# Threshold searches in groups of three tiles, two on ScalarE and one on VectorE

## The reference, cut to what matters

```
rel   = relu(einsum('bthd,bsd->bths', iq, ik_all))          # 8 index heads of 64
score = einsum('bths,bth->bts', rel, iw)
score = where(k_pos <= q_pos, score, -inf)
_, sel = lax.top_k(score, n_sel)                            # n_sel = min(256, t // 4)
```

## Time and profile before

| | us |
|---|---|
| median of 3 runs | 4327.86 |
| lowest and highest run | 4326.69, 4332.43 |
| the profiled execution's own time | 4345.04 |
| its span, first to last instruction | 4343.6 |
| channel block, from the trace's timeline | about 220 to 1,225 |

### The profile page before, as it was taken

One profiled execution on the slowest core, in us unless ns is written; L12 is line 12 of the kernel. 1 busy time (PEld: TensorE's weight loads), 2 busy tenths in 40 slices (PEclk: granted clock), 3 DMA queues, 4 the chain that ended last, 5 costly groups with the idle time before them and its releaser, 6 DMA issues. The chain is left out here.

```text
span 4343.6 us, 52016 instructions
## 1 busy us (share of the span) xinstructions
PE 3868.5 (89%) x19882; PEld 3152.5 (73%) x19882; DVE 2196.6 (51%) x4366; ACT 1532.5 (35%) x2446; POOL 653.1 (15%) x530
## 2 busy tenths in 40 slices
PE   7998887788859867888898889899999999979999
PEld 4554554455448546787887878799999999958787
DVE  6648988988953485343444334444444444320200
ACT  2135655565735333333333322322222222221211
POOL 0000000000000002322233210011111111034443
PEclk9998999999979678898899989999999999989999
DMA  3342212120142201111111124211112111064433
GB/s 112 93 98 56 77 43 72 34 72 30 49 145 89 80 9 45 32 37 27 44 39 45 32 66 136 83 40 49 49 39 59 39 48 49 29 209 136 131 121 108
DMA packets 287498, 298.52 MB, mean 69 GB/s; under 512 B 33871, under 2 KB 231375, under 8 KB 282410
## 3 DMA queue, kind: packets, MB, share of 16 engines
q1 hardware_dynamic: 264254, 249.46, 20.3%
q10 hardware_dynamic: 20944, 25.59, 1.7%
q0 software_dynamic: 2112, 20.97, 1.3%
HBM read 202.15 MB, written 94.10 MB: 68 GB/s over the span
## 5 line engine op out<-in xcount | busy, mean ns | idle before, releaser
L538 PE MATMUL chan_p_g<-ht,w_chan 128*128 128x412 f32 (+1 forms) x1760 | 677.4, 528 | 53.4 <-ACT chan_flat L586 33.7
L949 PE MATMUL up_p_g<-ht_high,up_wh 128*128 128x412 f32 (+1 forms) x1760 | 617.3, 351 | 0.0
L949 PE MATMUL up_p_g<-ht_low,up_wh 128*128 128x412 f32 (+1 forms) x1760 | 615.3, 350 | 0.0
L949 PE MATMUL up_p_g<-ht_high,up_wl 128*128 128x412 f32 (+1 forms) x1760 | 615.0, 349 | 0.0
L538 PEld LDWEIGHTS chan_p_g<-ht,w_chan 128*128 128x128 f32 x1760 | 341.5, 197 | 300.8 <-issue 233.4
L970 ACT ACTIVATE up_pre<-up_p_g 128x412 f32<-128x412 f32 (+1 forms) x220 | 113.2, 515 | 738.1 <-PE up_p_g L949 738.1
L1348 ACT ACTIVATE chan_signed<-chan_sc,chan_trial 128x512 bf16<-128x512 f32 (+6 forms) x224 | 304.9, 1361 | 148.6 <-DVE chan_trial L1403 127.8
L1038 DVE TENSOR_SCALAR up_acc<-up_pre,up_taps 128x2048 f32<-128x2048 f32 x44 | 59.3, 1347 | 557.4 <-ACT up_pre L970 557.4
L949 PEld LDWEIGHTS up_p_g<-ht_high,up_wh 128*128 128x128 f32 x1760 | 331.5, 188 | 1.6 <-POOL up_wl L1006 0.4
L949 PEld LDWEIGHTS up_p_g<-ht_low,up_wh 128*128 128x128 f32 x1760 | 331.3, 188 | 1.2
L949 PEld LDWEIGHTS up_p_g<-ht_high,up_wl 128*128 128x128 f32 x1760 | 331.2, 188 | 0.5
(11 more groups left out here) (561 smaller groups left out, 7042.6 us busy)
## 6 DMA issues: line engine op xcount, KB each, us to landing
down_a<-scratch_act SPq DMA_DIRECT2D x88, 512.0 KB, 3.7
scratch_act<-up_acc SPq DMA_DIRECT2D x22, 1028.0 KB
up_w<-in_w_up SPq DMA_DIRECT2D x44, 512.0 KB, 6.4
chan_iq<-scratch_iq SPq DMA_DIRECT2D x28, 512.0 KB, 7.2
scratch_qkv<-chan_acc SPq DMA_DIRECT2D x12, 1028.0 KB, 4.6
keys_of_raw<-scratch_qkv SPq DMA_DIRECT2D x16, 768.0 KB, 5.3
w_chan<-in_w_in SPq DMA_DIRECT2D x22, 512.0 KB, 4.5
proj_x<-in_x_prompt SPq DMA_DIRECT2D x16, 512.0 KB, 4.1
```

Of the source, the lines that this page charges most:

```text
L538: last = pe.matmul(p_g[u % BANKS][:, 0:cols.stop - cols.start], weights[:, k, :], K.ht[:, k, cols], start=(k == 0), stop=(k == KD - 1))
L949: last = pe.matmul(p_g[u][:, 0:cols.stop - cols.start], wp[s][:, k, :], hp[:, k, cols], start=(k == 0 and m == 0), stop=(k == KD - 1 and m ...
```

## The change

`Select` takes groups in place of pairs: `TRIPLES` is one group of two tiles and four of three. The first tile of each group is searched on VectorE, the one or two others on ScalarE, one Sign behind the other, with one signal after the last. The flags of ScalarE's tiles are formed in one operation against the constants in `bound`. `sc` has three buffers; the tile `signed`, to which the Sign wrote what nobody reads, is gone: the first Sign of a step writes to `left`, the second to `order`, which is half as long as before. So the running sum of a wide tile is made in two halves of at most 1,024 columns, the second against the rest of the limit. ScalarE waits for the stores of the group before ahead of its first Sign. `w_step` is set anew; the total of the weights is 859.5.

```diff
+TRIPLES = ((2, 3), (4, 5, 6), (7, 8, 9), (10, 11, 12), (13, 14, 15))
...
-        sel = Select(c, K, range(1, PAIRED), s_iqst, lambda t: (((t + 1) * P - 1) // WIDTH + 1) * 32)
+        sel = Select(c, K, TRIPLES, s_iqst, lambda t: (((t + 1) * P - 1) // WIDTH + 1) * 32)
...
-    RING = 3
+    RING, HALF = 3, SEQ // 2
...
-        self.sc = two("sc", [P, SEQ])
-        self.tie, self.signed = c.sb("tie", [P, SEQ], BF16), c.sb("signed", [P, SEQ], BF16)
-        self.order = c.sb("order", [P, SEQ])
-        self.left = c.sb("left", [P, SEQ], BF16)
+        self.sc = [c.sb(f"sc{i}", [P, SEQ]) for i in range(3)]
+        self.tie, self.left = c.sb("tie", [P, SEQ], BF16), c.sb("left", [P, SEQ], BF16)
+        self.order = c.sb("order", [P, self.HALF])
...
-    w_step = staticmethod(lambda p: 1.0 + 2.3 * (2 * p + 1) / 16)
+    w_step = staticmethod(lambda group: 0.8 + 2.2 * sum(t + 1 for t in group[1:]) / 16)
...
+            if q:
+                act.wait_ge(self.s_out, 16 * self.nth(group[0]))
             for m in range(32):
-                act.wait_ge(S["tried"], (p - self.pairs[0]) * 33 + m + 1)
-                act.activation(self.signed[:, 0:nk], self.sc[1][:, 0:nk], ACT.Sign, scale=-1.0,
-                               bias=self.trial[:, 1:2].bitcast(F32), accum_out=self.signs[:, :]).then_inc(S["signs"], 1)
-                yield self.w_step(p)
+                act.wait_ge(S["tried"], q * 33 + m + 1)
+                for b in range(1, len(group)):
+                    nk = (group[b] + 1) * P
+                    junk = self.left[:, 0:nk] if b == 1 else self.order[:, :].bitcast(BF16)[:, 0:nk]
+                    last = act.activation(junk, self.sc[b][:, 0:nk], ACT.Sign, scale=-1.0,
+                                          bias=self.trial[:, b:b + 1].bitcast(F32), accum_out=self.signs[:, b - 1:b])
+                last.then_inc(S["signs"], 1)
+                yield self.w_step(group)
...
+            for b in range(1, g):
+                dve.memset(self.bound[:, b - 1:b], float((group[b] + 1) * P - 2 * NSEL))
...
-                step(dve.tensor_scalar(miss[:, 1:2], signs[:, :], float(nb - 2 * NSEL), None, ALU.is_gt))
+                step(dve.tensor_tensor(miss[:, 1:g], signs[:, 0:g - 1], self.bound[:, 0:g - 1], ALU.is_gt))
...
-                    dve.scalar_tensor_tensor(out=trial[:, :], in0=miss[:, :], scalar=bit, in1=other[:, :],
+                    dve.scalar_tensor_tensor(out=trial[:, 0:g], in0=miss[:, 0:g], scalar=bit, in1=other[:, 0:g],
                                              op0=ALU.logical_shift_left, op1=ALU.bitwise_xor).then_inc(S["tried"], 1)
...
-                if b == 1:
+                if b:
...
-                step(dve.tensor_tensor_scan(order, tie, tie, 0.0, ALU.add, ALU.bypass))
-                step(dve.scalar_tensor_tensor(out=tie, in0=order, scalar=count[:, b:b + 1], in1=tie, op0=ALU.is_gt, op1=ALU.mult))
+                limit = count[:, b:b + 1]
+                for first in range(0, nk, self.HALF):
+                    part = self.tie[:, first:min(first + self.HALF, nk)]
+                    order = self.order[:, 0:min(self.HALF, nk - first)]
+                    step(dve.tensor_tensor_scan(order, part, part, 0.0, ALU.add, ALU.bypass))
+                    if first + self.HALF < nk:
+                        dve.tensor_tensor(self.rest[:, :], limit, self.order[:, self.HALF - 1:], ALU.subtract)
+                    step(dve.scalar_tensor_tensor(out=part, in0=order, scalar=limit, in1=part, op0=ALU.is_gt, op1=ALU.mult))
+                    limit = self.rest[:, :]
```

More of the change, by code:

```diff
@@ L1239, with __init__ @@
 class Select:
-    RING = 3
-    def __init__(self, c, K, pairs, stored, count):
-        self.c, self.K, self.pairs, self.stored, self.count_for = c, K, list(pairs), stored, count
+    RING, HALF = 3, SEQ // 2
+    def __init__(self, c, K, groups, stored, count):
+        self.c, self.K, self.groups, self.stored, self.count_for = c, K, groups, stored, count
+        self.of = [t for group in groups for t in group]
         two = lambda name, shape, dt=F32: [c.sb(f"{name}{b}", shape, dt) for b in range(2)]
@@ L1259, in __init__ @@
         self.s_iq, self.s_out = c.sems("sel_iq"), c.sem("sel_out")
-    def tiles(self):
-        return [(p, b, 2 * p + b) for p in self.pairs for b in range(2)]
     def units(self, t):
@@ L1267, in first @@
     def first(self, t):
-        return sum(len(self.units(u)) for _, _, u in self.tiles() if u < t)
+        return sum(len(self.units(u)) for u in self.of if u < t)
     def nth(self, t):
-        return t - 2 * self.pairs[0]
+        return t - self.of[0]
     cols = staticmethod(lambda t, kc: slice(kc * 512, min(kc * 512 + 512, (t + 1) * P)))
     w_score = staticmethod(lambda t, kc: 0.2 + 0.55 * (min(kc * 512 + 512, (t + 1) * P) - kc * 512) / 512)
-    w_step = staticmethod(lambda p: 1.0 + 2.3 * (2 * p + 1) / 16)
+    w_step = staticmethod(lambda group: 0.8 + 2.2 * sum(t + 1 for t in group[1:]) / 16)
     w_mask = staticmethod(lambda t: 1.0 + 12.7 * (t + 1) / 16)
     def total(self):
-        score = sum(self.w_score(t, kc) for _, _, t in self.tiles() for _, kc in self.units(t))
-        return score + sum(32 * self.w_step(p) for p in self.pairs) + sum(self.w_mask(t) for _, _, t in self.tiles())
+        score = sum(self.w_score(t, kc) for t in self.of for _, kc in self.units(t))
+        return score + sum(32 * self.w_step(group) for group in self.groups) + sum(self.w_mask(t) for t in self.of)
     def fetch(self, sp, t):
@@ L1288, in fetch @@
         for half in range(2):
-            sp.dma_start(self.iq[t % 2][half * ID:(half + 1) * ID, :, :, :].bitcast(F32).rearrange("d a h n -> d (a h) n"),
-                         self.K.d_iq2[:, :, :, t * P:(t + 1) * P].rearrange("a h d n -> d (a h) n")).then_inc(self.s_iq[t % 2], 16)
+            sp.dma_start(self.iq[self.nth(t) % 2][half * ID:(half + 1) * ID, :, :, :].bitcast(F32).rearrange("d a h n -> d (a h) n"),
+                         self.K.d_iq2[:, :, :, t * P:(t + 1) * P].rearrange("a h d n -> d (a h) n"))\
+              .then_inc(self.s_iq[self.nth(t) % 2], 16)
     def sync(self, sp):
         S = self.S
[L1294 to L1301, removed]
+        for t in self.of[:2]:
+            self.fetch(sp, t)
+        for group in self.groups:
+            for t in group:
+                for _, kc in self.units(t):
+                    yield self.w_score(t, kc)
+                if t + 2 <= self.of[-1]:
+                    self.fetch(sp, t + 2)
             for m in range(32):
-                yield self.w_step(p)
-            for b in range(2):
-                t = 2 * p + b
+                yield self.w_step(group)
+            for t in group:
                 yield self.w_mask(t)
@@ L1310, in finished @@
     def finished(self, sp):
-        sp.wait_ge(self.s_out, 32 * len(self.pairs))
+        sp.wait_ge(self.s_out, 16 * len(self.of))
     def tensor(self, pe):
         S = self.S
[L1315 to L1318, removed]
+        for group in self.groups:
+            for t in group:
+                b = self.nth(t) % 2
+                pe.wait_ge(self.s_iq[b], 32 * (self.nth(t) // 2 + 1))
                 for u, (h, kc) in enumerate(self.units(t)):
@@ L1327, in tensor @@
             for m in range(32):
-                yield self.w_step(p)
-            for b in range(2):
-                yield self.w_mask(2 * p + b)
+                yield self.w_step(group)
+            for t in group:
+                yield self.w_mask(t)
     def scalar(self, act):
         S = self.S
-        for p in self.pairs:
-            for b in range(2):
-                t = 2 * p + b
+        for q, group in enumerate(self.groups):
+            for t in group:
                 for u, (h, kc) in enumerate(self.units(t)):
@@ L1358, in vector @@
         step(dve.tensor_scalar(self.iw[:, :, :], K.small[:, :, 2 * GH + ID:], INDEX_SCALE, None, ALU.mult))
-        for p in self.pairs:
-            for b in range(2):
-                t = 2 * p + b
+        for q, group in enumerate(self.groups):
+            g = len(group)
+            for b, t in enumerate(group):
                 s = self.sc[b]
-                if self.nth(t) >= 2:
-                    dve.wait_ge(S["left"], self.nth(t) - b)
+                if q:
+                    dve.wait_ge(S["left"], self.nth(group[0]))
                 chunks = (t + 4) // 4
@@ L1381, in vector @@
                     yield self.w_score(t, kc)
[L1382 to L1385, removed]
+            na = (group[0] + 1) * P
+            dve.wait_ge(S["own"], self.nth(group[-1]) + 1)
+            for b in range(1, g):
+                dve.memset(self.bound[:, b - 1:b], float((group[b] + 1) * P - 2 * NSEL))
+            dve.memset(trial[:, 0:g].bitcast(F32), 0.0).then_inc(S["tried"], 1)
             for m in range(32):
@@ L1421, in vector @@
+                    step(dve.tensor_scalar(self.flip[:, :], trial[:, b:b + 1], 0x7F800000, None, ALU.bitwise_and))
```

36 lines of the change are left out of this document (17 added, 19 removed).

## The result

The changed kernel takes 4350.66 us (median of 7 runs, 4337.95 to 4358.14), the kernel before 4331.65 (7 runs, 4326.69 to 4338.56, the three shown above among them). The ratio is 1.0048 with a 95% interval of 1.0035 to 1.0061: slower by some 19 to 21 us, clear of noise. Forecast was +13 us and 4341 us. Of the 10 us between 4341 and 4351, 4 are the median of before, which rose from 4327.86 with four more runs.

The account below looks back on a forecast made before the run. The channel block was taken to last as long as its serial chain of score, search and mask. Searches +7, masks +10.7 and scoring −5 gave about +13 us on the 4327.86 median: 4341 us, range 4320 to 4370.

Parts of the forecast that it names:

- The step: Searches: a step lasts the sum of both ScalarE Signs plus 0.51 us, 4.41 us in the last group; searches +7 us.
- The cover: Searches: convolution parts beside the Signs stand out by 0.57 to 1.29 us each; 16 us where before 58.
- The masks: Mask stages on VectorE: more and wider corrections 6.3 us, eight running-sum splits 4.4 us; +10.7 us, nothing hides it.
- Scoring: Scoring stages: 3.5 us less projection, two fewer handovers from mask to scoring at 0.8 us each; −5 us.
- The sum: Channel block: searches +7, masks +10.7 and scoring −5 give about +13 us.
- A: Searches: second Sign waits for the first's accumulator read, evacuations may not fit the gap; 4353 to 4375 us; chance 0.17.
- B: Searches: convolution, Silu and starts beside the steps hide wholly; searches 481 us, total 4312 us; chance 0.13.
- D: Last two search groups: TensorE's clock falls to 1.2 GHz throughout; +145 us; chance 0.02.
- C: Mask to scoring: handovers cost 4.8 us each, two fewer give −9.6 us; sum +5, 4333 us; chance 0.18.

## Why the prediction was right

**The step.** It stands: sum of both Signs plus 0.51 us. 4.41 us were forecast and measured, and the five searches were forecast at about 42, 88, 105, 126 and 150 us and are 41.7, 88.5, 103.3, 124.6 and 150.0. The term was +7, it is +3.1: what stands out beside the steps came to 28 us after where 29 were forecast, the steps to 480 and not 481, and the cut of the earlier trace rows made before's searches 2 us too short, which went over into the masks.

**The cover.** Convolution parts stand out by 0.6 to 1.3 us in place of 2.5: shown by the pair of runs with narrow parts, 14.1 us for 19 large parts in place of 38.3. The evacuation lies in the gap before the next Sign, as the timeline shows.

**The masks.** This is the term that was mis-sized, +10.7 against +16.1. What was wrong in it is the count of convolution parts, large and first ones together: the prediction had six in the masks before and five after, and put the difference at nothing. The traces have four before (three large, one first) and six after (five and one). The large ones (L632) over the mask stages, after and then before:

```profile
sum 160.60, DVE 11.61; mean DVE 2.32
...
sum 144.50, DVE 6.96; mean DVE 0.99
```

That makes 4.7 us. The first mask's wait for its store is another 0.8. Less these, 10.6 are left for corrections and splits, as forecast (10.7), and the run with pairs measured 4.2 of it for the splits alone.

**Scoring.** −5 forecast, −5.1 measured, but not from the parts forecast, 3.5 us of projection and 1.6 of handovers. The projection matmuls (L538) in the scorings, before and after:

```profile
sum 297.40, PE 190.77 PEld 85.60; mean PE 27.25 PEld 12.23
...
sum 292.30, PE 180.80 PEld 79.62; mean PE 36.16 PEld 15.92
```

They are 442 and 420 records, 1.4 units fewer and not 0.6, and 10.0 us less of TensorE's time. TensorE's idle time in the scorings rose from 15.4 to 18.8 us, though two handovers are gone, and a projection record takes 0.43 us as before, so no clock was gained either. That the term came out at −5 is luck in its parts.

**The sum.** The block's 14.1 us lie close to the 13 forecast partly by luck as well: the searches were put 3.9 us too high and the masks 5.4 too low.

**The rivals.** A (a pair dearer than its sum) falls with the row at 1185.29, where the second Sign starts at the first one's end, 0.09 us before its accumulator read ends. Its own upper end was short: 4341 + 24 + 32 is 4397 and not 4375. B (all work beside hidden) falls with the searches at 508.1 us, where it had 481, and with the 14.1 us of convolution. D (TensorE's clock) falls: granted clocks of 0.94 to 0.99 in the searches, and at unit spacings of 7.2 us; the nearest to that limit was the run with a narrow second Sign, where it was full work and not the clock that held. C (a handover worth 4.8 us) falls with the idle time and the time of a record above. The median of all runs moved by 19 us and the block by 14; the interval reaches down to 15, and the unchanged stretch behind the block differs by up to 19 us between profiles, so nothing more can be read from that gap.

## What to carry to other kernels

When rounds of a serial search are merged over more tiles, fewer fixed costs are paid, but each round costs the sum of the columns on the engine that ends last; price that sum by both engines' rates per column before counting rounds. Where one engine has a single tile and time to spare, try giving it the widest one: here that took 16 us off the searches. Count also what the third tile asks for elsewhere: its buffer cost 4 us in the masks, the further corrections some 6. Work interleaved on an engine that ends early is partly hidden, here 22 of 36 us; in the stages where that engine is alone it costs its full time, so it is worth counting how many pieces of it fall there. Keeping them out of those stages was not tried.

## What the runs showed of the hardware

Two Sign instructions with accumulator outputs, one behind the other on ScalarE, run at the sum of their lengths: the read between them lies across the border (0.18 us, from 1185.20, and the next Sign from 1185.29), and in 32 pairs of 1,920 and 2,048 columns the means were 1.89 and 1.99 us. The median steps of all four groups of three, 2.48 to 4.41 us, are the sums of their Signs plus 0.51 us to within 0.02.

Given work without a gap, TensorE had a granted clock of 1.00 over the 119.6 us of the last search with the narrow second Sign. In the last search of the changed kernel, where it now and then waits for a bank, it was 0.95:

```profile
1145.03 11.25 PE L538 MATMUL chan_p_g<-ht,w_chan 128*128 128x408 f32 x32 [1.50 <-ACT chan_pre L582]
1159.81 10.61 PE L538 MATMUL chan_p_g<-ht,w_chan 128*128 128x412 f32 x25 [3.53 <-ACT chan_pre L582]
```
